# Chunks of the gate and up product: three groups of seven, weight sums by DMA, Silu in one operation

## The chip, the cores and the metric

One core of a Trainium2 chip runs the kernel. Its engines are TensorE (PE), VectorE (DVE), ScalarE (ACT), GpSimd (POOL) and SyncE (SP, which issues most DMAs); each works through its own program in order and waits on semaphores for the others. The metric is the device time of one execution in microseconds; lower is better.

## What is computed

Two transformer layers on 256 tokens of width 2048. Each layer mixes tokens (a sliding window attention in layer 0, a gated recurrence in layer 1, both with attention to 256 memory tokens) and then does a feed-forward step of width 5632, which is what matters here:

```python
x = x + jnp.concatenate([mix, mem_out], axis=-1) @ w_o[i]
gate, up = _split(rms_norm(x, norm_ffn[i]) @ w_gate_up[i], (D_FF, D_FF))
x = x + (jax.nn.silu(gate) * up) @ w_down[i]
```

All is float32.

## The kernel before

**Products.** A float32 product is made of three products of TensorE. Each operand is split in a high part (`_hi`, rounded to what TensorE takes in one pass) and a low part (`_lo`, the rest), and hi times hi, lo times hi and hi times lo are added in PSUM. ScalarE makes `w_hi` by a copy (L644), VectorE makes `w_lo` by a subtraction (L1104).

**Pieces.** Weights come as pieces of 256 rows by 512 columns (512 KB). SyncE loads a piece into one of eight slots of `raw` (`piece`, L411) when the piece eight before is used; `w_hi` has four slots (RING), so ScalarE can split piece n when piece n-4 is used; `w_lo` takes the place of the raw piece. TensorE counts `piece_used`. ScalarE and VectorE run LEAD = 3 pieces ahead: at step i of a loop over pieces they first do the extra work listed for step i and then split piece i+3. A plain piece is 12 products of 128x512 columns (2 row blocks, 3 parts, 2 token tiles; `plain_piece`, L1920).

**Chunks.** The gate and up product (`w_gate_up`) goes in chunks of 512 gate and 512 up columns. The first chunk is done by plain pieces before a loop. The other ten of a layer run in a loop of five turns with two chunks each (`half` 0 and 1). A chunk has 8 quads (row pair q, side 0 gate and side 1 up), thus 16 pieces.

**Groups of seven.** Quads 2 and 5 (SEVEN) are done with seven block products and not eight (`seven_products`, L1901): 21 products of TensorE for 24. It needs forms of the tokens (`seven_forms`, made once a layer, during the first chunk) and four sums of the weight blocks: two in `sums.two`, the third written over block 0 of the raw piece, and the fourth in `sums.all`. `seven_sums` (L1116) makes all four on VectorE; ScalarE waits for them before it splits the quad's first piece. `sums_high` and `sums_low` split the sums. TensorE wants `w_lo` of both pieces before a group, and counts both pieces used at its end.

**Banks.** The plain products and part of the sevens go to four PSUM banks (`own`), the rest of the sevens to the other four (`shared`). In the next chunk the two sets change roles. After the last group, at step 12, ScalarE copies `shared[0]` and both engines move a block of the result of the chunk before into `gT`; at step 13 `shared_products` (L1596) reads the shared banks and gives `own_free`, on which `chunk_products` (L1955) and `down_products` (L1938) wait before their first product. After the last piece `own_products` (L1608) reads the own banks and gives `shared_free`, on which the first group of the next chunk waits.

**Activation.** Silu of the gate is made by Tanh on ScalarE (step 2, L939), one operation for each tile on VectorE (`gate_silu`, step 4, L1581), and `times_up` (step 5, L1585): the product with up and a transpose in 32x32 blocks, which SyncE carries on with 16 small DMAs (`moved`) a chunk.

**GpSimd** makes the factors of the norms, and the masks of the recurrence of layer 1 early in the program. Much of the memory is used twice: `sum_all` is the tile `squares`, `down_two` is the tile `tanh_ff`.

## Time and profile before

| what | value |
|---|---|
| time, median of 3 runs | 2149.47 us (2149.44 to 2149.59) |
| the profiled execution, its own time | 2150.24 us |
| its span, first to last instruction | 2148.5 us |
| TensorE busy | 2135.4 us, 99% of the span |
| VectorE busy | 1682.8 us, 78% |
| ScalarE busy | 1119.4 us, 52% |
| GpSimd busy | 56.6 us, 3% |
| HBM read | 411.25 MB, 192 GB/s over the span |

Busy time tells which engine works most, not which one is waited for. An engine at 99% can only be helped by less work, and one at 78% can still hold the others up where its work comes in a lump. So the busy shares are read first, then windows of one chunk, then the timelines within it.

### The profile page before, as it was taken

The page shows a single profiled execution, that of the slowest core. Times are in us where ns is not written, and L with a number is a line of the kernel's source. Part 1 is how long each engine was busy: PE and PEld are TensorE (multiplying, and loading weights), DVE is VectorE, ACT ScalarE, POOL GpSimd, SP SyncE. Part 2 cuts the span into 40 slices and gives each one's busy share as a digit, 9 for nine tenths or more (in the row PEclk, how much of TensorE's full clock was granted, in tenths as well). Part 3 has the DMA queues.
Part 4 walks back from the last instruction along what each step waited for, and adds up shares of the span by engine and source line. Part 5 has one row for each costly group of instructions (what it writes and reads, how often), then busy time and mean ns, then how long its engine had stood idle before and what let it go on. Part 6 is the DMA issues. An engine that isn't in the chain of part 4 may idle for free.

```text
span 2148.5 us, 29147 instructions
## 1 busy us (share of the span) xinstructions
PE 2135.4 (99%) x9992; PEld 1777.8 (83%) x9992; DVE 1682.8 (78%) x2139; ACT 1119.4 (52%) x1478; POOL 56.6 (3%) x99
## 2 busy tenths in 40 slices
PE   8999999999999999999999999999999999999999
PEld 7888888888888888888888888888888888888887
DVE  6657766898988898777666767667989898898775
ACT  7755654555455555454544544455554555555453
POOL 2101100000000000000000000000000000000000
PEclk9999999999999999999999999999999999999999
DMA  9765467667666766675665656577676667666664
GB/s 327 243 197 147 132 211 207 206 203 227 209 205 201 232 207 211 191 226 180 212 175 158 197 159 199 163 222 205 203 224 210 200 209 227 208 210 202 227 199 138
DMA packets 244568, 435.56 MB, mean 203 GB/s; under 512 B 23040, under 2 KB 43648, under 8 KB 244480
## 3 DMA queue, kind: packets, MB, share of 16 engines
q1 hardware_dynamic: 243392, 432.31, 65.1%
q10 hardware_dynamic: 1088, 2.10, 0.3%
q8 instruction: 52, 0.85, 0.2%
q14 instruction: 36, 0.29, 0.0%
HBM read 411.25 MB, written 2.10 MB: 192 GB/s over the span
## 4 chain that ended last, share of the span: by engine, by line
PE 99%; ACT 0%; DVE 0%; DMA 0%; issue 0%; DVEq 0%; SPq 0%; ACTq 0%
PE unit_bank L1886 30%; PE mix_bank L1928 24%; PE unit_bank L1928 24%; PE mix_bank L1898 7%; PE unit_bank L1898 7%; PE mix_bank L1886 4%; PE mix_bank L1979 1%; PE mix_bank L2109 1%; PE mix_bank L2044 0%; PE mix_bank L2006 0%; PE mix_bank L2053 0%; PE mix_bank L2095 0%; DVE w_lo L1104 0%; PE mix_bank L2017 0%; PE mix_bank L2028 0%; DMA source_T<-in_mem_T 0%
## 5 line engine op out<-in xcount | busy, mean ns | idle before, releaser
L644 ACT ACTIVATE w_hi<-raw 128x1024 fp32r<-128x1024 f32 x767 | 798.1, 1057 | 828.2 <-DVE sum_all L1128 166.5
L1104 DVE TENSOR_TENSOR w_lo<-raw,w_hi 128x1024 fp32r<-128x1024 f32 x767 | 923.4, 1221 | 353.0 <-ACT w_hi L644 346.8
L1886 PE MATMUL unit_bank<-w_hi,hT_hi 128*128 128x512 f32 (+1 forms) x576 | 181.2, 396 | 0.0
L1886 PE MATMUL unit_bank<-w_hi,hT_lo 128*128 128x512 f32 (+1 forms) x576 | 176.2, 387 | 0.0
L1886 PE MATMUL unit_bank<-w_lo,hT_hi 128*128 128x512 f32 (+1 forms) x576 | 175.9, 387 | 0.0
L1928 PE MATMUL unit_bank<-w_lo,hT_hi 128*128 128x512 f32 x480 | 147.9, 389 | 0.0
L1928 PE MATMUL mix_bank<-w_lo,hT_hi 128*128 128x512 f32 x480 | 147.8, 389 | 0.0
L1928 PE MATMUL mix_bank<-w_hi,hT_hi 128*128 128x512 f32 x480 | 147.8, 389 | 0.0
L1928 PE MATMUL unit_bank<-w_hi,hT_hi 128*128 128x512 f32 x480 | 147.8, 389 | 0.0
L1928 PE MATMUL unit_bank<-w_hi,hT_lo 128*128 128x512 f32 x480 | 147.8, 389 | 0.0
L1928 PE MATMUL mix_bank<-w_hi,hT_lo 128*128 128x512 f32 x480 | 147.7, 389 | 0.0
L1886 PEld LDWEIGHTS unit_bank<-w_hi,hT_lo 128*128 128x128 f32 x576 | 107.9, 188 | 21.7
L1886 PEld LDWEIGHTS unit_bank<-w_lo,hT_hi 128*128 128x128 f32 x576 | 107.9, 188 | 21.7
L1886 PEld LDWEIGHTS unit_bank<-w_hi,hT_hi 128*128 128x128 f32 x576 | 104.5, 188 | 18.2 <-DVE w_lo L1104 0.2
L1928 PEld LDWEIGHTS mix_bank<-w_hi,hT_hi 128*128 128x128 f32 x480 | 90.1, 188 | 18.7
L1928 PEld LDWEIGHTS unit_bank<-w_hi,hT_hi 128*128 128x128 f32 x480 | 90.1, 188 | 18.7
L1928 PEld LDWEIGHTS unit_bank<-w_lo,hT_hi 128*128 128x128 f32 x480 | 90.1, 188 | 18.7
L1928 PEld LDWEIGHTS mix_bank<-w_lo,hT_hi 128*128 128x128 f32 x480 | 90.1, 188 | 18.7
L1928 PEld LDWEIGHTS unit_bank<-w_hi,hT_lo 128*128 128x128 f32 x480 | 90.1, 188 | 18.7
L1928 PEld LDWEIGHTS mix_bank<-w_hi,hT_lo 128*128 128x128 f32 x480 | 90.1, 188 | 18.7
L1928 PE MATMUL mix_bank<-w_hi,gT_lo 128*128 128x512 f32 x272 | 83.8, 389 | 0.0
L1928 PE MATMUL unit_bank<-w_hi,gT_lo 128*128 128x512 f32 x272 | 83.8, 389 | 0.0
(427 smaller groups left out, 3602.7 us busy)
## 6 DMA issues: line engine op xcount, KB each, us to landing
raw<-in_w_gate_up SPq DMA_DIRECT2D x352, 512.0 KB, 4.4
raw<-in_w_down SPq DMA_DIRECT2D x176, 512.0 KB, 4.6
raw<-in_w_in_b SPq DMA_DIRECT2D x104, 512.0 KB, 3.7
raw<-in_w_o SPq DMA_DIRECT2D x64, 512.0 KB, 3.8
raw<-in_w_in_a SPq DMA_DIRECT2D x40, 512.0 KB, 3.7
moved<-turned SPq DMA_DIRECT2D x528, 32.0 KB, 2.5
raw<-in_w_mem_kv SPq DMA_DIRECT2D x31, 512.0 KB, 5.5
tanh_ff<-act_ff SPq DMA_DIRECT2D x112, 32.0 KB, 3.0
```

The costliest lines, as they stand in the source:

```text
L644: act.activation(w_hi[:, s, :, :], raw[:, r, :, :], ACT.Copy).then_inc(sems["hi_ready"], 1)
L1104: dve.tensor_tensor(w_lo[:, r, :, :], raw[:, r, :, :], w_hi[:, s, :, :].bitcast(F32), ALU.subtract).then_inc(sems["lo_ready"], 1)
L1886: ins = pe.matmul(all_banks[2 * pair + tile][:, 0:cols], stationary[part][:, kt + j, tile * P:(tile + 1) * P], b[:, j, 0:cols], start=open ...
L1898: ins = pe.matmul(bank[:, :], x_parts[part], w, start=start and m == 0, stop=stop and m == 2)
L1928: ins = pe.matmul(own[2 * tile + side][:, :], x[part][:, kt + j, tile * P:(tile + 1) * P], w, start=opens and j == 0 and m == 0, stop=clos ...
L1979: ins = pe.transpose(mix_bank[b][:, n * P:(n + 1) * P], src[:, n * width:(n + 1) * width], ident[:, :])
L2109: ins = pe.matmul(mix_bank[b][:, h * P:(h + 1) * P], early_key[:, h, :], whole(query_in, h * P + half, (4 * P - half, TILES), (size, block ...
```

## The change

- SEVEN is (2, 4, 6): three groups of seven in a chunk, and a chunk ends with one plain quad. The order of the row pairs is QUAD_KTS, so that the third group has rows 10 and 11.
- Two of a group's four weight sums are no longer made by VectorE. SyncE loads block 0 into both halves of a `two` tile (`spread`, two DMAs of 256 KB), GpSimd issues two DMAs that add another block onto them (`chunk_weight_sums`). The tile exists twice now, and groups take turns. Of the quad's first piece only the lower half is loaded into `raw`.
- VectorE makes the third sum (`third_sum`) and the fourth (`fourth_sum`), both a step later than `seven_sums` did. ScalarE waits for the third before its split and for the fourth before `sums_high`.
- The work that follows the last group goes from steps 12 and 13 to 14 and 15 (LAST_SEVEN).
- Silu is one operation of ScalarE; `gate_silu` of VectorE is gone. The half factors are gone too.
- The forms of the third group (`late_form`) are made at steps 11 and 12 of the first chunk, in memory that the masks have later; GpSimd makes the masks between layer 0 and layer 1 instead, and the recurrence waits for them (`masks_ready`).
- SyncE waits for the forms (`own_free`) before it starts on the loop.

```diff
--- before.py
+++ after.py
 LEAD = 3
 LEVELS = 7
+OWN_FREED = CHUNKS_FF + 2
 QUAD_PIECES = 2
 CHUNK_PIECES = KT
-SEVEN = (2, 5)
-SEVEN_APART = 6
+SEVEN = (2, 4, 6)
+SEVEN_APART = 4
+QUAD_KTS = (0, 2, 4, 6, 8, 12, 10, 14)
+SPREAD_STEPS = (1, 5, 13)
+LAST_SEVEN = 2 * SEVEN[-1] + 2
 SEVEN_PIECES = tuple(2 * q for q in SEVEN)
...
+        late_forms = tuple(at(f"late_forms_{n}", [3, P], F32R, place[0] - LEVELS * SEQ // 2 * 4 + m * 3 * P * 4)
+                           for m, n in enumerate(("hi", "lo")))
...
-        chunk_sums = Sums(sums, sums_lo, sum_all, sum_all_lo, sums_hi)
+        chunk_sums = tuple(Sums(two, two_lo, sum_all, sum_all_lo, sums_hi)
+                           for two, two_lo in ((sums, sums_lo), (down_two, down_two_lo)))
+        chunk_forms = [tuple(f[:, g, :, :] for f in forms) for g in range(2)]
+        chunk_forms.append(tuple(f[:, :, :] for f in late_forms))
...
+        def chunk_sum(half, n):
+            return (half * len(SEVEN) + n) % 2
...
+            def lower_half_piece(w, kt, col):
+                s = slot[0] % RAW
+                slot[0] += 1
+                t.move("piece_used")
+                sp.wait_ge(sems["piece_used"], t.value("piece_used", RAW))
+                sp.dma_start(raw[:, s, 1, :], w[(kt + 1) * P:(kt + 2) * P, bass.ds(col, COLS)]).then_inc(sems[f"arrived{s}"], 16)
+
+            def spread(w, kt, col, b, used):
+
+                sp.wait_ge(sems["piece_used"], t.value("piece_used", used))
+                for m in range(2):
+                    sp.dma_start(chunk_sums[b].two[:, m, :], w[kt * P:(kt + 1) * P, bass.ds(col, COLS)]).then_inc(sems[f"spread{b}"], 16)
...
+                before = [2 * q + 2 - CHUNK_PIECES for q in SEVEN] + [2 * q + 2 for q in SEVEN]
+                spread_after = [before[len(SEVEN) + m - 2] for m in range(len(SEVEN))]
...
+                sp.wait_ge(sems["own_free"], layer * OWN_FREED + 1)
                 with t.loop(0, CHUNKS_FF // 2, {"piece_used": 2 * CHUNK_PIECES, "turned_ready": 2}) as j:
                     for half in range(2):
+                        col = j * (2 * COLS) + (1 + half) * COLS
                         for n in range(CHUNK_PIECES):
-                            piece(wg, n // 2 * 2, j * (2 * COLS) + (1 + half) * COLS + n % 2 * D_FF)
+                            load = lower_half_piece if n in SEVEN_PIECES else piece
+                            load(wg, QUAD_KTS[n // 2], col + n % 2 * D_FF)
+                            if n in SPREAD_STEPS:
+                                m = SPREAD_STEPS.index(n)
+                                spread(wg, QUAD_KTS[SEVEN[m]], col, chunk_sum(half, m), n + 1 - spread_after[m])
                             chunk_turns(n)
...
+            def chunk_weight_sums(layer):
+
+                w = w_gate_up[layer, :, :]
+                with t.loop(0, CHUNKS_FF // 2, {f"spread{b}": 32 * len(SEVEN) for b in range(2)}) as j:
+                    for half in range(2):
+                        col = j * (2 * COLS) + (1 + half) * COLS
+                        for n, q in enumerate(SEVEN):
+                            kt, b = QUAD_KTS[q], chunk_sum(half, n)
+                            pool.wait_ge(sems[f"spread{b}"], t.next(f"spread{b}", 32))
+                            pool.dma_start(chunk_sums[b].two[:, 0, :], w[(kt + 1) * P:(kt + 2) * P, bass.ds(col, COLS)],
+                                           accum_op=ALU.add).then_inc(sems[f"summed{b}"], 16)
+                            pool.dma_start(chunk_sums[b].two[:, 1, :], w[kt * P:(kt + 1) * P, bass.ds(col + D_FF, COLS)],
+                                           accum_op=ALU.add).then_inc(sems[f"summed{b}"], 16)
...
+                def gate_silu():
                     for s in range(TILES):
                         act.wait_ge(sems["gate_sum"], t.next("gate_sum"))
-                        act.activation(tanh_ff[:, s, :], act_ff[:, s, :], ACT.Tanh,
-                                       scale=half_rs[:, s:s + 1]).then_inc(sems["tanh_ff_ready"], 1)
-
-                def chunk(j, shared):
+                        act.activation(act_ff[:, s, :], act_ff[:, s, :], ACT.Silu,
+                                       scale=rs[:, s:s + 1]).then_inc(sems["silu_ready"], 1)
+
+                def chunk(j, half, shared):
                     for i in pieces(CHUNK_PIECES):
                         if i + LEAD in SEVEN_PIECES:
-                            act.wait_ge(sems["sum_ready"], t.next("sum_ready", 3))
+                            act.wait_ge(sems["sum_ready"], t.next("sum_ready"))
                         if i + LEAD - 2 in SEVEN_PIECES:
-                            sums_high(chunk_sums)
+                            act.wait_ge(sems["sum_ready"], t.next("sum_ready"))
+                            sums_high(chunk_sums[chunk_sum(half, SEVEN_PIECES.index(i + LEAD - 2))])
                         if i == 2:
-                            gate_tanh()
-                        if i == 12:
+                            gate_silu()
+                        if i == LAST_SEVEN:
                             act.wait_ge(sems["piece_used"], t.value("at"))
                             act.activation(up_ff[:, 0, :], shared[0][:, :], ACT.Copy).then_inc(sems["first_copied"], 1)
-                        if i == 12:
+                        if i == LAST_SEVEN:
                             moved_block(gT, j * 4)
...
+            def third_sum(sums, b):
+
+                r = slot[0] % RAW
+                blocks = four_blocks(raw, r)
+                dve.wait_ge(sems[f"summed{b}"], t.next(f"summed{b}", 32))
+                dve.wait_ge(sems[f"arrived{r}"], t.value(f"arrived{r}", -16))
+                dve.tensor_tensor(blocks[:, 0, :], sums.two[:, 1, :], blocks[:, 1, :], ALU.add).then_inc(sems["sum_ready"], 1)
+
+            def fourth_sum(sums, used):
+
+                r = slot[0] % RAW
+                blocks = four_blocks(raw, r)
+                dve.wait_ge(sems["piece_used"], t.value("at", used))
+                dve.wait_ge(sems[f"arrived{r + 1}"], t.value(f"arrived{r + 1}", -16))
+                dve.wait_ge(sems["sum_ready"], t.next("sum_ready"))
+                dve.tensor_tensor(sums.all[:, :], blocks[:, 0, :], blocks[:, 3, :], ALU.add).then_inc(sems["sum_ready"], 1)
+                dve.wait_ge(sems["sum_ready"], t.next("sum_ready"))
...
                 def times_up():
-                    dve.wait_ge(sems["dve_chain"], t.next("dve_chain"))
                     dve.wait_ge(sems["shared_free"], t.value("shared_free"))
                     for s in range(TILES):
+                        dve.wait_ge(sems["silu_ready"], t.next("silu_ready"))
                         ins = dve.scalar_tensor_tensor(out=up_ff[:, s, :], in0=up_ff[:, s, :],
-                                                       scalar=half_rs2[:, s:s + 1], in1=tanh_ff[:, s, :], op0=ALU.mult,
+                                                       scalar=rs[:, s:s + 1], in1=act_ff[:, s, :], op0=ALU.mult,
                                                        op1=ALU.mult)
...
-                def chunk(j, own, shared):
+                def chunk(j, half, own, shared):
 
                     for i in pieces(CHUNK_PIECES):
-                        if i + LEAD + 1 in SEVEN_PIECES:
-                            seven_sums(chunk_sums)
+                        if i + LEAD in SEVEN_PIECES:
+                            n = SEVEN_PIECES.index(i + LEAD)
+                            b = chunk_sum(half, n)
+                            third_sum(chunk_sums[b], b)
+                            fourth_sum(chunk_sums[b], i - (2 * SEVEN[n - 1] + 2) if n else 0)
                         if i + LEAD - 2 in SEVEN_PIECES:
-                            sums_low(chunk_sums)
-                        if i == 4:
-                            gate_silu()
+                            sums_low(chunk_sums[chunk_sum(half, SEVEN_PIECES.index(i + LEAD - 2))])
                         if i == 5:
                             times_up()
-                        if i == 12:
+                        if i == LAST_SEVEN:
                             moved_block(gT, j * 4, "gT_ready")
-                        if i == 13:
+                        if i == LAST_SEVEN + 1:
                             shared_products(shared)
                     own_products(own)
...
-                    if i == 10:
+                    if i == 9:
                         seven_forms()
+                    if i == 11:
+                        seven_forms_lo()
+                        late_form()
                     if i == 12:
-                        seven_forms_lo()
+                        late_form_lo()
...
-            def chunk_products(own, shared):
+            def chunk_products(half, own, shared):
 
                 pe.wait_ge(sems["own_free"], t.next("own_free"))
                 for q in range(CHUNK_PIECES // 2):
                     if q in SEVEN:
                         n = SEVEN.index(q)
-                        seven_products(hT, 2 * q, forms, n, chunk_sums, own, shared, n == 0, n == len(SEVEN) - 1, evicted)
+                        seven_products(hT, QUAD_KTS[q], chunk_forms[n], chunk_sums[chunk_sum(half, n)], own, shared, n == 0, n == len(SEVEN) - 1, evicted)
                         continue
                     for side in range(2):
-                        plain_piece(hT, 2 * q, side, own, q == 0, q == CHUNK_PIECES // 2 - 1)
+                        plain_piece(hT, QUAD_KTS[q], side, own, q == 0, q == CHUNK_PIECES // 2 - 1)
...
```

In `seven_products` only the arguments are other. `late_form` is one operation of 512 columns and four of 128 on VectorE, and `late_form_lo` two more.

## Rows read from the trace of the kernel before

**Rows 1.** The page: its head, and busy time by engine.
```profile
span 2148.5 us, 29147 instructions
...
PE 2135.4 (99%) x9992; PEld 1777.8 (83%) x9992; DVE 1682.8 (78%) x2139; ACT 1119.4 (52%) x1478; POOL 56.6 (3%) x99
```

**Rows 2.** Windows: stretch, length, busy of PE, PEld, DVE, ACT, POOL; PEclk, DMA, GB/s.
```profile
414.19:456.35 42.16, 42.16 (x188) 34.91 (x186) 37.38 (x43) 21.84 (x25) 0.00 (x0) 1.00 0.69 213
```

**Rows 3.** Timeline, TensorE, one chunk: start, length, engine, line, operation, count.
```profile
429.83 0.62 PE L1928 MATMUL mix_bank<-w_hi,hT_hi 128*128 128x512 f32 x2
...
440.71 0.39 PE L1898 MATMUL mix_bank<-w_hi,hT_hi 128*128 128x512 f32 x1
...
445.47 0.62 PE L1928 MATMUL mix_bank<-w_hi,hT_hi 128*128 128x512 f32 x2
...
456.35 0.62 PE L1928 MATMUL unit_bank<-w_hi,hT_hi 128*128 128x512 f32 x2
```

**Rows 4.** Timeline, VectorE, the same chunk.
```profile
429.61 1.41 DVE L1589 SCALAR_TENSOR_TENSOR up_ff<-up_ff,half_rs,tanh_ff 128x512 f32<-128x512 f32 x2
432.28 1.18 DVE L1104 TENSOR_TENSOR w_lo<-raw,w_hi 128x1024 fp32r<-128x1024 f32 x1
433.39 1.22 DVE L1123 TENSOR_TENSOR sums<-raw 128x1024 f32<-128x1024 f32 x1
434.64 0.69 DVE L1126 TENSOR_TENSOR raw<-sums,raw 128x512 f32<-128x512 f32 x1
435.37 0.69 DVE L1128 TENSOR_TENSOR sum_all<-raw 128x512 f32<-128x512 f32 x1
...
446.76 1.23 DVE L1104 TENSOR_TENSOR w_lo<-raw,w_hi 128x1024 fp32r<-128x1024 f32 x1 [2.98 <-ACT w_hi L644]
447.90 1.29 DVE L1209 TENSOR_TENSOR gT_lo<-moved,gT_hi 128x512 f32 x2
449.23 1.23 DVE L1104 TENSOR_TENSOR w_lo<-raw,w_hi 128x1024 fp32r<-128x1024 f32 x1
450.37 0.68 DVE L1600 TENSOR_TENSOR act_ff<-unit_bank,up_ff 128x512 f32<-128x512 f32 x1
452.42 0.69 DVE L1605 TENSOR_TENSOR act_ff<-unit_bank,up_ff 128x512 f32<-128x512 f32 x1
...
456.63 1.29 DVE L1613 TENSOR_TENSOR act_ff<-mix_bank,act_ff 128x512 f32<-128x512 f32 x2
```

**Rows 5.** Groups by line, whole span: busy us, mean ns, idle before.
```profile
L1134 DVE TENSOR_TENSOR sums_lo<-sums,sums_hi 128x1024 fp32r<-128x1024 f32 x40 | 49.0, 1226 | 5.9 <-ACT sums_hi L658 4.8
...
L1581 DVE SCALAR_TENSOR_TENSOR tanh_ff<-tanh_ff,act_ff 128x512 f32<-128x512 f32 x44 | 28.3, 686 | 0.0
```

**Rows 6.** Timeline, ScalarE, the same chunk.
```profile
445.67 1.06 ACT L644 ACTIVATE w_hi<-raw 128x1024 fp32r<-128x1024 f32 x1 [3.70 <-PE mix_bank L1898]
...
447.11 1.15 ACT L707 ACTIVATE gT_hi<-moved 128x512 f32 x2
```

**Rows 7.** Start of the span: window of the first products; timeline, two rows.
```profile
7.98:13.24 5.26, 5.26 (x12) 4.12 (x13) 3.95 (x8) 4.01 (x8) 0.00 (x0) 1.00 1.03 408
...
7.14 0.69 DVE L1440 TENSOR_TENSOR w_lo<-raw,w_hi 128x512 fp32r<-128x512 f32 x1
...
7.98 1.19 PE L1886 MATMUL unit_bank<-w_hi,memT_hi 128*128 128x512 f32 x2 [7.98 <-DVE w_lo L1440]
```

**Rows 8.** SyncE's queue: timeline; DMA issues by size; landings of line 432.
```profile
430.16 0.99 SPq L417 DMA_DIRECT2D raw<-in_w_gate_up  x2
...
raw<-in_w_mem_kv SPq DMA_DIRECT2D x2, 256.0 KB, 3.8
...
DMA to landing us min/median/max: 1.8/2.6/5.4
```

**Rows 9.** Timeline, GpSimd: its longest operation and a small one.
```profile
232.37 2.90 POOL L581 TENSOR_TENSOR head_rs<-head_ms,minus_half 128x16 f32<-128x16 f32 x1
...
1052.87 1.11 POOL L579 TENSOR_SCALAR head_ms<-head_ss 128x8 f32<-128x8 f32 x1 [21.52 <-DVE head_ss L1214]
```

108 lines of the change are left out of this document (63 added, 45 removed).

## The prediction

> **What bounds the kernel now.** I read the page first: TensorE is busy for 2135.4 of 2148.5 us, VectorE for 78% and ScalarE for 52% [rows 1]. A busy TensorE can still be waiting, so I then cut one half turn of the chunk loop out with the windows view. In 42.16 us TensorE has no idle time at full granted clock, VectorE is busy 37.38 us, ScalarE 21.84, and the DMA engines 0.69 at 213 GB/s [rows 2]. The timeline of TensorE gives the borders [rows 3]: four plain pieces take 440.71 - 429.83 = 10.88 us (48 products, 0.2267 us each), a group of seven takes 445.47 - 440.71 = 4.76 us (21 products), and the last four plain pieces 10.88 us. A chunk is 186 products, 186 x 0.2267 = 42.16 us. So here the number of products sets the time, and the other engines matter only where one of their chains is longer than the TensorE work that covers it. Those chains are what I looked for next, in the timelines of VectorE and ScalarE.
>
> The execution I work from has a span of 2148.5 us [rows 1] and a time of its own of 2150.24 us, so 1.7 us lie around the span; the median of the three runs, 2149.47, is 0.8 us (0.04%) below it. The change leaves what is around the span alone, so the differences from this execution are added to the median.
>
> **What is taken away.** A third group of seven replaces the two plain pieces of one quad: 21 products for 24, in 20 chunks (10 a layer). That is 3 x 0.2267 = 0.68 us a chunk and 13.6 us in all, on the path. A chunk would need 183 x 0.2267 = 41.48 us.
>
> **VectorE's balance.** Per chunk it loses two sums of 1024 columns (433.39 to 434.64, 1.25 us each [rows 4]) and two silu operations of 0.69 [rows 5]: some 3.8 us. It gains for the third group two sums of 512 columns (0.73 us each [rows 4]) and the low halves (1.23 [rows 5] and one more of 512 columns, about 0.6): 3.3 us. So 37.4 becomes about 36.9 of 41.48 us: no bound by quantity. ScalarE gains one pair of sums_high, some 1.6 us by the same sizes, on 21.8, and changes Tanh for Silu at the same shape. Neither counts. What counts is order.
>
> **First new wait: the banks at the end of a chunk.** The two halves of PSUM change roles: what was `shared` in one chunk is `own` in the next, and `chunk_products` waits on `own_free` before its first product. VectorE gives `own_free` with the last operation of `shared_products` (L1605), which can only start after the last group of seven. Before, the last group (q=5) is followed by four plain pieces, 10.88 us of cover. After, SEVEN ends in 6: two plain pieces, 24 x 0.2267 = 5.44 us. `moved_block` and `shared_products` move with it, from steps 12 and 13 to 14 and 15, in the same order. I call G the start of the piece behind the last group, 445.47 [rows 3]. ScalarE may split the piece four behind the group's first only now (ring of four), at 445.67 [rows 6]. VectorE's low half of it starts at 446.76, then the two gT_lo operations at 447.90 (they need ScalarE's from 447.11 [rows 6]), the next low half at 449.23, the four sums of shared_products from 450.37, the last starting at 452.42 and taking 0.69: done at 453.11 = G + 7.64 [rows 4]. VectorE stood idle before 446.76, so this chain hangs on G, not on a backlog, and it moves with the group. From VectorE's result to TensorE's first product I take 0.15 us: L1440 ends at 7.14 + 0.69 = 7.83, TensorE starts at 7.98 [rows 7]. So the next chunk starts at G + 7.79 and not at G + 5.44: **2.35 us of idle TensorE a chunk**. It comes after each of 20 chunks, since `down_products` waits on `own_free` too. Bounds: 2.2 (no latency) to 2.6 us.
>
> **Second new wait: the ninth piece.** The groups are now at pieces 4, 8 and 12. At step 5 VectorE does third_sum and fourth_sum for piece 8, then `times_up` (two products, two transposes), then the low half of piece 8, and at step 6 that of piece 9. `sum_all` exists once, and `fourth_sum(..., i - (2*SEVEN[n-1]+2))` gives -1 here: it waits until the first group (pieces 4, 5) is used. Everything named stands behind it in VectorE's order. Call that time T, 429.83 [rows 3]. VectorE is known to start 456.63 - 456.35 = 0.28 us after such an event [rows 3, 4]. Then: fourth_sum 0.73 (435.37 minus 434.64), times_up and transposes 432.28 - 429.61 = 2.67, low half of piece 8 433.39 - 432.28 = 1.11, and that of piece 9 with its full length, 1.23 [rows 4]: T + 6.02, with the latency T + 6.17. TensorE has two plain pieces to do, 5.44 us, and then wants both halves at once (`lo_ready` by 2). **0.73 us of idle TensorE a chunk.** In the kernel before, times_up began at 429.61, before T. Bounds: 0.3 (VectorE starts and TensorE wakes at once) to 1.0. At the third group (step 9) the same wait costs nothing: without times_up, VectorE needs 0.28 + 0.73 + 1.11 + 1.23 = 3.35 of 5.44 us.
>
> **The adding DMAs.** No row shows a DMA issued by GpSimd or one that adds. Their deadline is tightest for the third group: SyncE can issue pieces 12 and 13 only at T (430.16, two in 0.99 us [rows 8]), then two spreads of 256 KB, until about T + 2.4; a 256 KB load landed in 3.8 us at the busy start [rows 8], so T + 5.8. GpSimd waits for that, and issues two DMAs. VectorE must begin third_sum by T + 12.0: the group starts at T + 6.17 + 4.76 + 5.44 = T + 16.37, and before it lie third_sum 0.7, two ScalarE splits of about 1.0, the last low half 1.23 and 0.15, or 4.2 with the hand-overs. That leaves 6.2 us. From below: one GpSimd operation of 1.11 and a landing of 1.8; from above: two of 2.90 and a landing of 5.4, 11.2 us, late by 5 us a chunk [rows 8, 9]. I take 1 us for each issue (the small one, since only an issue is queued and nothing computed) and a landing like the load's 3 to 4: 5 to 6 us, just in time, at no cost. A miss costs its full length 20 times, since VectorE stands at third_sum with all splits behind it. The first and second groups have over 5 us more.
>
> The Trainium skill (DMA: Bandwidth & Descriptors, Anatomy of one DMA) puts a GpSimd DMA at about 2.0 us plus the bytes at 436 GB/s, an estimate of 2.6 us for 256 KB; by it the sums would be in time too. It also says that adding is left to GpSimd's DMAs, and no run here shows either yet.
>
> The bytes: a chunk moves 16 x 512 KB = 8.4 MB now; it gains 3 x 3 x 256 KB net (two spreads and two adds less the half that isn't loaded), 2.4 MB, and the adds read their target also, 1.6 MB. 12.4 MB in 44.5 us is 280 GB/s; the first microseconds ran at 408 [rows 7]. Not a bound.
>
> **Around the loop.** The extra form (`late_form`) lies in steps 11 and 12 of the plain chunk with over 1 us to spare each; the new wait of SyncE on `own_free` delays the first loads of the loop, 0 to 0.5 us a layer. The masks moved on GpSimd are 28 small operations, by the small one [rows 9] at most 31 us, and are wanted 17 pieces, 46 us, into the group that follows. I take 0.5 us for all, 0 to 3.
>
> **Sum.** Per chunk 2.35 + 0.73 - 0.68 = +2.40 us, times 20 = +48.0, plus 0.5: 2149.5 + 48.5 = **2198 us**, 2.3% slower. The period should be 44.56 us instead of 42.16. Bounds of the two waits alone: 2.5 to 3.6 a chunk, 2186 to 2208.
>
> **Rivals.**
> 1. The adding DMAs are late. The same sum plus 20 times the miss: at 1 us 2218, at 2.5 us 2248, at the upper bound 2298. For it: 6.2 us for two unseen operations. Against it: spare DMA bandwidth.
> 2. The cover holds after all (the faster side). The mechanism is the chain behind the last group: if VectorE gave the banks back within 5.3 us instead of 7.64, and times_up ran before the wait, the gain of 0.68 a chunk stays: 2149.5 - 13.6 = 2136. It turns at waits of 0.68 us a chunk in sum. Against it: neither order is in the diff. With only the second wait left, 2149.5 + 20 x (0.73 - 0.68) = 2150, no change.
> 3. TensorE's clock falls after the 2.35 us holes. After its first idle 7.98 us twelve products took 5.26 us, 0.44 each instead of 0.23, as at 1.2 GHz, though the column reads 1.00 [rows 7]. If every hole cost that again, 5.26 - 12 x 0.2267 = 2.5 us a chunk: 2198 + 51 = 2249. Behind that start all holes of the span sum to 2148.5 - 7.98 - 2135.4 = 5.1 us, so its rows can't tell what a hole of 2.35 us does, and the first one was over three times as long. The skill's page TensorE: Matmul & The Clock Gate (Part 1) says that an idle array drops to the lower clock and regains it by work; by it this rival would need holes longer than mine.
> 4. GpSimd is held off by VectorE while it makes its DMAs. That is rival 1 with another cause. The skill (SBUF — State Buffer, Door 1 to 3, the trap under them) describes descriptor making that stops while VectorE copies in a two-port mode; the loop has no such copy, so by the page there is nothing, and no row here shows it.
>
> **How the numbers follow.** Forecast (both waits, DMAs in time) 0.60. DMAs late 0.27, of it half below 2230. Clock 0.05. Only one of the two waits (2183 or 2150) 0.05, cover holds 0.03. Range: from 2186, just under the bounds of the forecast, to 2250, which takes in the clock rival and late DMAs up to 2.5 us; left out are some 0.08 below and 0.08 above. A difference under 0.2% (4.3 us) can't be told from none. Faster by more: 0.03; within: 0.03; slower: 0.94.
>
> **What the profile after would show.** TensorE idle of 2.3 us before the first product of each chunk, released by L1605's successor (act_ff or up_ff of shared_products), 20 times; idle of 0.7 us before the middle group, released by w_lo, 20 times; period 44.6 us; clock 1.00; VectorE near 83% of a period. If third_sum waits on a DMA with TensorE idle before the third group, rival 1 holds, and its length is the miss. If the period is 41.5, I have misread who waits for the banks. A period between 41.5 and 44 would say that one chain is shorter than its rows.

## The result and the profile after

The changed kernel takes **2320.7 us** (median of 4 runs, 2319.4 to 2327.8) where the kernel before takes 2149.5: a ratio of 1.080, 95% interval 1.079 to 1.082. Slower was forecast, but 2198 us, with a range of 2186 to 2250. So the sign was right and 123 us are missing from the sum.

The page of the changed kernel, head, busy time and the queue of GpSimd's DMAs (packets, MB, share):

```profile
span 2317.7 us, 30023 instructions
...
PE 2182.6 (94%) x9932; PEld 1789.3 (77%) x9932; DVE 1675.1 (72%) x2149; ACT 1174.7 (51%) x1543; POOL 161.2 (7%) x215
...
q0 software_dynamic: 17280, 31.46, 8.8%
```

Against [rows 1], TensorE's busy time went up by 47.2 us though it has 60 products less, which should have saved 13.6: **60.8 us of slower products**, at a lower clock or at the edges of holes. Its idle time went from 13.1 to 135.1: **122.0 us of new holes**. Together 122.0 + 60.8 - 13.6 = 169.2, all that the span grew by. Where the holes are, by the view of TensorE's waits (us in total, times, longest):

```profile
PE unit_bank L1989 <- DVE w_lo L1159: 44.7, 22, 7.2
PE mix_bank L1989 <- DVE w_lo L1159: 33.1, 20, 3.6
PE unit_bank L2019 <- DVE act_ff L1670: 21.7, 10, 2.3
PE mix_bank L2019 <- DVE act_ff L1670: 21.6, 10, 2.2
```

L2019 is the plain product and L1670 the last operation of `shared_products`: the wait for the banks, 43.3 us in 20. L1989 is the group of seven: 77.8 us in 42. One chunk tells them apart, in the timelines of TensorE, VectorE, SyncE and GpSimd:

```profile
430.10 0.73 PE L2019 MATMUL mix_bank<-w_hi,hT_hi 128*128 128x512 f32 x2 [2.15 <-DVE act_ff L1670]
...
432.18 1.06 PE L2019 MATMUL mix_bank<-w_hi,hT_hi 128*128 128x512 f32 x2
433.04 1.06 PE L2019 MATMUL mix_bank<-w_hi,hT_lo 128*128 128x512 f32 x2
...
453.62 0.50 PE L1989 MATMUL mix_bank<-w_hi,hT_hi 128*128 128x512 f32 x1 [0.55 <-DVE w_lo L1159]
...
467.05 0.50 PE L1989 MATMUL mix_bank<-w_hi,hT_hi 128*128 128x512 f32 x1 [2.94 <-DVE w_lo L1159]
...
481.34 0.72 PE L2019 MATMUL unit_bank<-w_hi,hT_hi 128*128 128x512 f32 x2 [2.17 <-DVE act_ff L1670]
```
```profile
447.75 0.69 DVE L1201 TENSOR_TENSOR sum_all<-raw 128x512 f32<-128x512 f32 x1 [1.93 <-PE mix_bank L1989]
...
462.74 0.69 DVE L1192 TENSOR_TENSOR raw<-down_two,raw 128x512 f32<-128x512 f32 x1 [5.17 <-DMA down_two<-in_w_gate_up]
```
```profile
448.94 0.82 SPq L443 DMA_DIRECT2D down_two<-in_w_gate_up  x2
```
```profile
454.17 0.87 POOL L624 DMA_DIRECT2D down_two<-in_w_gate_up  x1 [20.92 <-DMA down_two<-in_w_gate_up]
454.81 1.12 POOL L626 DMA_DIRECT2D down_two<-in_w_gate_up  x1
```

The chunk lasts 481.34 - 430.10 = 51.24 us where 44.56 were forecast. The hole of 2.17 us at its end and that of 0.55 before the middle group were forecast. The hole of **2.94 us before the third group** was not, nor were the products 0.43 us apart from 431.3 to 434.2 (432.18 to 433.04 are two). With T = 447.46, the first group's end: the spreads go out at T + 1.5, GpSimd starts at T + 6.7 and ends at T + 8.5, VectorE gets the sums at T + 15.3. The deadline was T + 12.0. TensorE's row names `w_lo` only because it waits for that; VectorE itself stands for 5.17 us at `third_sum`, on the DMA.

The granted clock, by the windows view (length, busy of PE, PEld, DVE, ACT, POOL, PEclk, DMA, GB/s), shows the slow stretches of this chunk behind its two long holes, and none behind the short one:

```profile
430.10:442.70 12.60, 12.60 (x48) 10.28 (x49) 10.89 (x13) 5.77 (x7) 1.76 (x2) 0.86 0.79 207
...
453.62:458.51 4.89, 4.89 (x21) 4.05 (x22) 3.95 (x4) 0.54 (x1) 1.77 (x2) 1.00 0.62 134
...
467.05:471.60 4.55, 4.55 (x13) 3.58 (x14) 4.10 (x4) 1.86 (x2) 0.51 (x1) 0.65 1.03 379
```

At the two levels a product takes 0.2267 and 0.427 us (2.4 and 1.2 GHz). Not every long hole has slow products behind it. In TensorE's timeline of the whole span 25 of the 62 holes in the loops have them: 12 of the 20 at the banks, 11 of the 20 before the third group, and both at the loops' entries; of the 20 of 0.55 and 0.65 us none has. Where they follow, they are 5 to 11 and cost some 1.7 us, 41 us in sum. Most of the other 20 of the 60.8 us are the edges of the 62 holes: the product before a hole and the one behind it take 0.3 us more together.

### The profile page after: what moved, and what is told of

It is laid out like the page before. It is cut to its first block, busy times and chain, and to the rows that moved or that the text cites. A ratio compares the mean times of both kernels' runs of the same rounds, so it can differ in the third digit from the quotient of the medians.

```text
span 2317.7 us, 30023 instructions
## 1 busy us (share of the span) xinstructions
PE 2182.6 (94%) x9932; PEld 1789.3 (77%) x9932; DVE 1675.1 (72%) x2149; ACT 1174.7 (51%) x1543; POOL 161.2 (7%) x215
## 3 DMA queue, kind: packets, MB, share of 16 engines
q0 software_dynamic: 17280, 31.46, 8.8%
## 4 chain that ended last, share of the span: by engine, by line
PE 71%; DMA 11%; issue 5%; DVE 5%; ACT 4%; SPq 2%; ACTq 0%; DVEq 0%; POOLq 0%; POOL 0%
PE unit_bank L1977 27%; PE mix_bank L2019 14%; PE unit_bank L2019 11%; DMA sums<-in_w_gate_up 7%; PE unit_bank L1989 7%; PE mix_bank L1989 7%; DMA down_two<-in_w_gate_up 4%; PE mix_bank L1977 3%; ACT w_hi L692 2%; DVE w_lo L1159 2%; PE mix_bank L2070 1%; ACT gT_hi L755 1%; PE mix_bank L2200 1%; DVE raw L1192 1%; DVE act_ff L1665 1%
## 5 line engine op out<-in xcount | busy, mean ns | idle before, releaser
L2019 PE MATMUL mix_bank<-w_hi,hT_hi 128*128 128x512 f32 x400 | 128.5, 403 | 21.6 <-DVE act_ff L1670 21.6
L2019 PE MATMUL unit_bank<-w_hi,hT_hi 128*128 128x512 f32 x400 | 125.8, 396 | 17.8 <-DVE act_ff L1670 17.5
L2019 PE MATMUL mix_bank<-w_hi,hT_lo 128*128 128x512 f32 x400 | 127.7, 402 | 0.0
L2019 PE MATMUL mix_bank<-w_lo,hT_hi 128*128 128x512 f32 x400 | 126.8, 399 | 0.0
L2019 PE MATMUL unit_bank<-w_hi,hT_lo 128*128 128x512 f32 x400 | 125.3, 395 | 0.0
L2019 PE MATMUL unit_bank<-w_lo,hT_hi 128*128 128x512 f32 x400 | 124.9, 394 | 0.0
L1977 PEld LDWEIGHTS unit_bank<-w_hi,hT_lo 128*128 128x128 f32 x576 | 107.9, 188 | 21.8
L1977 PEld LDWEIGHTS unit_bank<-w_hi,hT_hi 128*128 128x128 f32 x576 | 104.4, 188 | 18.2 <-DVE w_lo L1159 0.2
L2019 PEld LDWEIGHTS mix_bank<-w_hi,hT_hi 128*128 128x128 f32 x400 | 76.8, 194 | 41.5 <-issue 25.8
L2019 PEld LDWEIGHTS unit_bank<-w_hi,hT_hi 128*128 128x128 f32 x400 | 75.2, 190 | 37.3 <-issue 20.8
L2019 PEld LDWEIGHTS mix_bank<-w_lo,hT_hi 128*128 128x128 f32 x400 | 78.2, 195 | 16.9
L2019 PEld LDWEIGHTS mix_bank<-w_hi,hT_lo 128*128 128x128 f32 x400 | 77.7, 194 | 16.8
L2019 PEld LDWEIGHTS unit_bank<-w_lo,hT_hi 128*128 128x128 f32 x400 | 76.5, 191 | 16.2
L2019 PE MATMUL unit_bank<-w_hi,gT_hi 128*128 128x512 f32 x272 | 84.8, 393 | 4.2 <-DVE act_ff L1670 4.2
L2019 PEld LDWEIGHTS unit_bank<-w_hi,hT_lo 128*128 128x128 f32 x400 | 76.1, 190 | 16.1
L2019 PE MATMUL unit_bank<-w_lo,gT_hi 128*128 128x512 f32 x272 | 85.1, 394 | 0.0
```

The source lines that it names most:

```text
L1977: ins = pe.matmul(all_banks[2 * pair + tile][:, 0:cols], stationary[part][:, kt + j, tile * P:(tile + 1) * P], b[:, j, 0:cols], start=open ...
L2019: ins = pe.matmul(own[2 * tile + side][:, :], x[part][:, kt + j, tile * P:(tile + 1) * P], w, start=opens and j == 0 and m == 0, stop=clos ...
```

## The experiments

The kernel before ran beside each of them (medians 2150.1 to 2150.4).

**Remove one suspected cause at a time.** In e1 the third group's four sums are VectorE's again and its piece is loaded whole; the other groups keep the adding DMAs:

```diff
-SPREAD_STEPS = (1, 5, 13)
+SPREAD_STEPS = (1, 5)
+BY_DMA = len(SPREAD_STEPS)
...
-                            third_sum(chunk_sums[b], b)
+                            if n < BY_DMA:
+                                third_sum(chunk_sums[b], b)
+                            else:
+                                two_sums(chunk_sums[b])
```

> The changed kernel, but the third group's four weight sums are made by VectorE as before (its first piece is loaded whole, no spreads and no adding DMAs for it; groups one and two keep theirs). Theory A (adding DMAs late for the third group only, 3.3 us a chunk by the idle of TensorE before the third group, and about half of the slow clock behind that hole): 2321 - 20 x 3.3 - about 23 = 2230 us, no idle of TensorE before the third group, the holes of 2.2 us (banks) and 0.6 us (middle group) stay. Theory B (GpSimd's DMAs disturb everything, by their bytes or by holding VectorE): four of six remain, so only a third of the excess goes, some 2290 us. Theory C (the VectorE work that comes back, 1.25 us a chunk, opens a new wait): above 2235 us with VectorE busy in front of the third group.

Measured: 2258.6 us (1.050, 1.048 to 1.051), 62 less: between theories A and B. It has no hole before the third group, and those at the banks and before the middle group stay. What theory A missed is new: ten holes before the first group, 15.3 us in sum, and 17.3 us at the loops' entries for 13.5. GpSimd now leaves up to 8.1 us between the two adding DMAs of a pair, 99.5 us in 15 pairs; this comes back in e4.

In e2 `shared_products` comes ahead of gT's block:

```diff
                         if i == LAST_SEVEN:
+                            shared_products(shared)
+                        if i == LAST_SEVEN + 1:
                             moved_block(gT, j * 4, "gT_ready")
-                        if i == LAST_SEVEN + 1:
-                            shared_products(shared)
```

> The changed kernel with two steps of VectorE swapped at the end of a chunk: shared_products (which gives the banks back) at step 14 and the gT move at step 15. Theory A (TensorE waits for the banks because the chain behind the last group is 7.64 us against 5.44 us of cover): the chain becomes 7.64 - 1.33 - 1.14 = 5.2 us plus 0.15 latency, so the hole of 2.2 us goes 20 times, 47 us, and the slow clock behind it, about 23: 2250 us. If the clock does not hang on this hole: 2274 us. Rival (VectorE or the adding DMAs are the bound and the banks' hole would be filled by a later wait): under 10 us of gain, above 2310 us.

Measured: 2295.7 us (1.066, 1.063 to 1.069), only 25 less; its own rival (above 2310) falls too. The view of waits says where the rest went:

```profile
PE unit_bank L1989 <- DVE w_lo L1159: 66.6, 30, 6.7
PE mix_bank L1989 <- DVE w_lo L1159: 41.9, 30, 3.0
```

The 43.3 us at the banks are gone, but the waits before groups of seven grew from 77.8 to 108.5, with 18 new ones: a hole in front of the first group (0.9 and 2.4 us in two chunks). It seems that the hole at the banks had given VectorE and the DMAs time for that group.

In e3 `times_up` stands between the third and the fourth sum; in the change it stands behind both:

```diff
                             third_sum(chunk_sums[b], b)
+                            if i == 5:
+                                times_up()
                             fourth_sum(chunk_sums[b], i - (2 * SEVEN[n - 1] + 2) if n else 0)
...
-                        if i == 5:
-                            times_up()
```

> The changed kernel with times_up between third_sum and fourth_sum at step 5, so that it runs before the wait for the first group and not behind it. Theory A (waits follow each other in one chain: the adding DMAs of the third group start at T, when the first group is used, and land at T + 15.3 whatever happens between): the hole before the middle group, 0.6 us, goes, and the one before the third group grows by as much: no change, 2320 us within 5. Rival (the holes simply add): 20 x 0.7 = 14 us less, 2307 us.

Measured: 2300.5 us (1.070, 1.067 to 1.073). The waits on `w_lo` fall from 77.8 to 65.8 us, the 20 holes of 0.6. It gained 20 us, more than the 12 of the holes and more than both theories, though one of its four runs (2294.4 to 2307.7) lies at the rival's 2307. The holes before the third group are hardly longer for it (53 us for 52), so theory A's one chain is wrong and the rival, that the holes add, is right. The other 7 us are TensorE's busy time: some 6 by the edges of 20 holes at 0.3, and little by the clock (193 slow products for 201).

e4 has all three edits:

> All three edits: the third group's sums on VectorE, shared_products before the gT move, times_up before the wait. Theory A (two orders and one late transfer explain the whole loss, and the slow clock follows from the holes): no holes in the loop, granted clock 1.00, and the gain in products is left: 2149.5 - 13.6 + 0 to 3 = 2136 to 2139 us. Rival (the third group costs more on VectorE than the three products save, or the clock falls for another reason): 2150 us or more.

Measured: 2239.9 us (1.042, 1.040 to 1.044), a miss by 100 us. The holes at the banks and before the third group are gone and those before the middle group are down to 0.2 us, but another stands there, 51.2 us in 10 waits before the first group, the two at the loops' entries (5.84 and 11.03 us) among them; in the other chunk of a turn it is 0.9 to 2.7 us. Timelines of GpSimd and VectorE, and GpSimd's waits:

```profile
461.51 0.87 POOL L625 DMA_DIRECT2D sums<-in_w_gate_up  x1 [31.04 <-DMA sums<-in_w_gate_up]
468.80 0.86 POOL L627 DMA_DIRECT2D sums<-in_w_gate_up  x1 [6.42 <-issue]
```
```profile
474.89 0.69 DVE L1204 TENSOR_TENSOR raw<-sums,raw 128x512 f32<-128x512 f32 x1 [2.09 <-DMA sums<-in_w_gate_up]
```
```profile
POOL sums L627 <- issue: 58.1, 9, 7.6
POOL down_two L627 <- issue: 44.0, 10, 5.9
```

GpSimd gives out the second adding DMA of a pair 6.4 us after the first ends, with nothing to wait for. That is 102 us in 19 of 40 pairs.

**Take the DMAs, or only the adding, away.** In e5 VectorE makes all sums; it is e4 with

```diff
-SPREAD_STEPS = (1, 5)
+SPREAD_STEPS = ()
...
-            chunk_weight_sums(0)
...
-            chunk_weight_sums(1)
```

> The changed kernel with all three reorderings of the run e4_all_three, and no adding DMA at all: VectorE makes the four weight sums of all three groups from pieces that are loaded whole. Theory A (in e4_all_three only the adding DMAs of the first two groups are left as a cause of holes, and the holes as the cause of the lower clock): no hole, 183 products of 0.2267 us a chunk, about 2138 us (2134 to 2146), TensorE busy 2122. Rival B (VectorE, about 41 us of work in 41.5, becomes the bound once it makes all sums): 2160 or more, with holes released by w_lo and none of VectorE's own waits on DMAs.

Measured: 2243.5 us (1.043, 1.042 to 1.045). Rival B holds: without one adding DMA it is no faster than e4. Now VectorE is late for the first group, in part because it waits for ScalarE's split behind silu:

```profile
475.65 1.28 ACT L986 ACT_TABLE_LOAD   x1
476.94 1.33 ACT L986 ACTIVATE act_ff<-act_ff,rs 128x512 f32<-128x512 f32 x2
```
```profile
479.25 1.22 DVE L1158 TENSOR_TENSOR w_lo<-raw,w_hi 128x1024 fp32r<-128x1024 f32 x1 [2.37 <-ACT w_hi L691]
```

e6 is e4, and e7 the changed kernel, with the addition left out of the same DMAs:

```diff
-                            pool.dma_start(chunk_sums[b].two[:, 0, :], w[(kt + 1) * P:(kt + 2) * P, bass.ds(col, COLS)],
-                                           accum_op=ALU.add).then_inc(sems[f"summed{b}"], 16)
+                            pool.dma_start(chunk_sums[b].two[:, 0, :], w[(kt + 1) * P:(kt + 2) * P, bass.ds(col, COLS)]).then_inc(sems[f"summed{b}"], 16)
```

> e4_all_three with GpSimd's DMAs plain copies and not adding (the two sums then lack their first block). Theory A (adding is what makes the transfer slow): the landing falls from about 6 to about 3.6 us and VectorE finds the sums ready: some 2195 to 2210. Rival B (GpSimd gives the second DMA of a pair out 3 to 7 us after the first, whatever it does): the gap between the two stays, 2230 to 2240.

> The changed kernel itself with GpSimd's DMAs plain copies and not adding (the sums lack their first block). Theory A (adding makes the landing 5 to 7 us, and that is the hole before the third group): landing near 3.6, the hole of 2.9 us falls to under 1 and part of the slow products after it goes: 2235 to 2270. Rival B (the chain is long by the order of its steps and the busy queues, not by the addition): less than 15 us gained, above 2305.

Measured: e6 2208.7 us (1.027, 1.025 to 1.029), 31 less than e4, and the 6 us gaps are gone (0.6 us from one DMA to the next). e7 2243.8 us (1.044, 1.043 to 1.046), 77 less; of the 20 holes before the third group 3 are left, 3.2 us in sum. The bytes from HBM are the same, so the addition as such costs, in both. Its price, by the DMA issues of 400 to 900 us in e7 (count, KB, median us to landing), and by its page:

```profile
sums<-in_w_gate_up POOLq DMA_DIRECT2D x28, 256.0 KB, 3.5
down_two<-in_w_gate_up POOLq DMA_DIRECT2D x28, 256.0 KB, 3.7
...
q0 software_dynamic: 9600, 31.46, 4.3%
```

In the changed kernel the same two rows say 5.4 and 5.3, the packets are 17280 for the same bytes, and one issue takes 0.87 to 1.09 us where a plain one takes 0.56.

e8 is the kernel before with the work behind the last group two steps later on both engines, as in the change (VectorE's part):

```diff
-                        if i == 12:
+                        if i == 14:
                             moved_block(gT, j * 4, "gT_ready")
-                        if i == 13:
+                        if i == 15:
                             shared_products(shared)
```

> The kernel before, with gT's block at step 14 and shared_products at step 15 and nothing else: the first wait by itself, at 186 products a chunk. The hole should be the 2.2 to 2.4 us of the changed kernel. Theory A (a hole costs its own length only): 2149.5 + 20 x 2.3 = 2195. Theory C (each such hole also lowers TensorE's clock for the next products, as the 8 products 0.427 us apart in the changed kernel suggest, 8 x 0.2 = 1.6 us): 2195 + 32 = 2227.

Measured: 2180.6 us (1.014, 1.012 to 1.016), below both. The hole is 1.22 us, not 2.3. The last group is two pieces earlier here, so VectorE's chain need not wait for its end; that is argued from the order, not tried. All 20 cost 30 us, 1.5 each, and the clock stays at 1.00: a hole of this length costs itself and some 0.3 us in the products at its edges. What a hole of 2.3 us does to the clock, the question between the two theories, e8 can't say.

**Silu.** e12 is the kernel before with silu in one operation and nothing else; e14 has it at step 1, before ScalarE's wait for the first group's sums:

```diff
+                        if i == 1:
+                            gate_tanh()
                         if i + LEAD in SEVEN_PIECES:
                             act.wait_ge(sems["sum_ready"], t.next("sum_ready", 3))
...
-                        if i == 2:
-                            gate_tanh()
```

> The kernel before with silu in one operation of ScalarE and no gate_silu on VectorE, and nothing else. Theory A (this part is off the path, as forecast): 2149 to 2151. Rival B (the loads of ScalarE's table, two a turn, delay the fifth piece as in e5_no_adding): 2155 or more.

> e12_silu_alone with silu at step 1, ahead of ScalarE's wait for the first group's sums. Theory A (the 6.6 us of e12_silu_alone are the 10 holes of 0.4 us released by the fifth piece, behind table load and silu): 2150 to 2152, equal to the kernel before. Rival B (silu on ScalarE costs in another way): still 2155 or more.

Measured: e12 2156.9 us (1.003, 1.002 to 1.004), so 6.6 us lost, and e14 2150.4 us (1.000, 0.999 to 1.001), none. With Tanh ScalarE loads no table in the loop. With Silu it has two loads a turn, each 1.28 us, 20 in all: one right before silu, one before a split near the turn's end. At step 2 the first lies, with silu, between the splits of pieces 4 and 5. The Trainium skill (ScalarE: Activation LUTs, What ACT_TABLE_LOAD costs) says some 1283 ns for the load and 1380 ns more for a drain; the trace agrees with the first and shows no drain, since silu starts at once after the load, as in e5's rows.

**Repairing VectorE's order.** e10 is e5 with silu at step 4; e11 gives the middle group's two sums back to adding DMAs; e9 adds gT's block at step 13 in the first chunk of each turn; e13 has silu at step 1 instead of 4.

```diff
-                        if i == 2:
+                        if i == 4:
                             gate_silu()
...
-                        if i == LAST_SEVEN + 1:
+                        if i == (LAST_SEVEN + 1 if half else LAST_SEVEN - 1):
                             moved_block(gT, j * 4, "gT_ready")
```

> e5_no_adding with ScalarE's silu at step 4 and not at step 2, that is behind the splits of the first group's two pieces. In e5_no_adding a load of ScalarE's table (1.28 us) and two silu operations (1.33 in sum) stand between the splits of pieces 4 and 5, and VectorE waits 2.37 us for the second, in one of two chunks. Theory A (that wait is part of the hole before the first group): the holes of 3.6 and 2.2 us there become 1.4 and 1.0, with less lost to the clock: 2200 to 2222. Rival B (VectorE has too much work between the last group and the first, and silu's place is nothing): above 2235.

> e10_silu_later, with the two sums of the middle group alone given back to SyncE's spreads and GpSimd's adding DMAs; the first and third group stay with VectorE. Theory A (an adding DMA is harmless where its group has over 10 us of time, and takes 1.2 us from VectorE just where it is late): the hole of 1.4 us before the middle group goes, 25 us less than e10_silu_later, 2170 to 2195. Rival B (the adding DMAs also stall here, 6 us between the two of a pair): no gain on e10_silu_later.

> e11_middle_by_dma, with gT's block at step 13 in the first of a turn's two chunks (in the second its memory is still used by the sums), where VectorE stands idle for 2.9 us behind the third group. Theory A (VectorE's backlog between the third group and the next first group is the hole): 1.2 us less in 10 of 20 chunks, 8 to 12 us below e11_middle_by_dma. Rival B (the hole before the first group hangs on ScalarE or a DMA): the same as e11_middle_by_dma within 3 us.

> e9_eased with ScalarE's silu at step 1, ahead of its wait for the first group's sums, where ScalarE stands idle for 7 us in every chunk. Theory A (silu and the table load before it delay the seventh piece, then times_up, in one of two chunks, and so make the hole of 1.65 us before the middle group): that hole goes, 10 x 1.6 us less, 2165 to 2172. What is left is the hole of 1.2 us before the first group in one of two chunks. Rival B (the holes of the second chunk of a turn come from VectorE's backlog alone): 2180 to 2186.

Measured: e10 2234.6 (1.040, 1.038 to 1.041), e11 2194.6 (1.021, 1.019 to 1.022), e9 2184.0 (1.015, 1.014 to 1.017) and e13 2167.3 us (1.008, 1.006 to 1.009). For e10 the gain is only 9 us, near its rival: silu moved the lateness on to the middle group (2.9 us in one of two chunks). The other three are in theory A's ranges, e11 with a gain of 40 us where 25 were named. In e13 only 12.0 us of holes before groups are left, and still a chunk without one lasts 42.0 us and not 41.48. Before its middle group, with VectorE's low halves for it last:

```profile
565.68 0.61 PE L2034 MATMUL unit_bank<-w_lo,hT_hi 128*128 128x512 f32 x2
566.27 0.50 PE L2004 MATMUL unit_bank<-w_hi,hT_hi 128*128 128x512 f32 x1
566.61 0.39 PE L2004 MATMUL unit_bank<-w_hi,hT_lo 128*128 128x512 f32 x1
```
```profile
563.86 2.36 DVE L1160 TENSOR_TENSOR w_lo<-raw,w_hi 128x1024 fp32r<-128x1024 f32 x2
```

Two products should take 0.45 us and take 0.59, and the next takes 0.34 for 0.23: 0.25 us lost at the border without idle time in the rows. The trace says why: the second low half ends at 566.22 and TensorE starts at 566.27, 0.05 us behind it, so this is a short wait for `w_lo`. From 380 to 800 us in e13 every border before a first or middle group is like this, while before the third group the low half is ready 0.95 us early or more and nothing is lost.

**Repairing SyncE's order.** e15 is the changed kernel with one number changed, so that the third group's spreads go out ahead of pieces 12 and 13:

```diff
-SPREAD_STEPS = (1, 5, 13)
+SPREAD_STEPS = (1, 5, 11)
```

> The changed kernel, with the third group's spreads issued by SyncE ahead of pieces 12 and 13 and not behind them. Theory A (the chain spread, landing, adding DMAs, landing is the hole before the third group, link by link): about 1 us less of a hole of 2.9 us in 20 chunks, 2320.7 - 20 to - 40 = 2281 to 2301. Rival B (the landings depend on what else moves at that time, so an earlier issue lands no earlier): above 2312.

Measured: **2233.7 us** (1.039, 1.037 to 1.040), 87 less. One window of a whole chunk, and the links in the timelines of SyncE, GpSimd and VectorE:

```profile
426.14:470.94 44.80, 42.08 (x183) 34.19 (x184) 36.85 (x43) 24.40 (x28) 5.27 (x6) 1.00 0.86 251
```
```profile
442.25 0.82 SPq L443 DMA_DIRECT2D down_two<-in_w_gate_up  x2
```
```profile
446.25 0.87 POOL L624 DMA_DIRECT2D down_two<-in_w_gate_up  x1 [15.01 <-DMA down_two<-in_w_gate_up]
```
```profile
453.78 0.69 DVE L1192 TENSOR_TENSOR raw<-down_two,raw 128x512 f32<-128x512 f32 x1 [1.75 <-DMA down_two<-in_w_gate_up]
```

T is 441.92 here: issue at T + 0.3, GpSimd at T + 4.3, sums at T + 11.9. The issue is 1.2 us sooner and the end 3.4, and all 20 holes before the third group are gone. The spreads, no longer behind the 768 KB of the two pieces, landed in 4.0 us for 5.2, and the adding DMAs in 5.8 for 6.8, though they are still issued behind those pieces. So neither theory is quite right: the chain holds link by link, but its landings depend on the place in the queue. TensorE's idle time fell by 52.5 us and its busy time by 32.6, with 8 holes that slow products follow for 25.

e16 has the repairs of e2, e3 and e15, silu at step 1, and the first group's spreads ahead of the chunk's first piece; e17 is e4 with the last two.

```diff
+                        spread(wg, QUAD_KTS[SEVEN[0]], col, chunk_sum(half, 0), -spread_after[0])
                         for n in range(CHUNK_PIECES):
```

> The changed kernel with every repair that the runs so far point to, all three groups' sums still by adding DMAs: shared_products ahead of gT, times_up ahead of the fourth sum, silu at step 1, and the spreads of the first and third group issued ahead of the pieces that come free with them. Theory A (order is all that was wrong): no hole over 0.5 us, 183 products of 0.2267 us a chunk, 2136 to 2148, faster than the kernel before. Rival B (with the holes at a chunk's start gone, GpSimd's second adding DMA of a pair is given out 6 us late, as in e4_all_three, and the first group waits for it): 2170 to 2230.

> e4_all_three with silu at step 1 and the first group's spreads issued ahead of the chunk's first piece. Theory A (the first group's sums came late because its spreads stood behind two pieces in SyncE's order, and silu did the rest): the hole of 5 us before the first group goes, 2136 to 2150. Rival B (the gap of 6 us between the two adding DMAs of the first pair stays whatever SyncE does): at least half of the loss stays, above 2185.

Measured: e16 2182.4 (1.015, 1.014 to 1.017) and e17 2176.5 us (1.013, 1.011 to 1.014). e16 is in its rival's range, but not by its mechanism: GpSimd issues both DMAs of every pair at once. There all adding DMAs land later (medians 7.4 and 6.8 us from 400 to 900 us), and small holes remain; that they meet more pieces is my guess. e17 lies between the theories: the gaps between two adding DMAs are still there, 141 us in sum, but mostly hidden.

No version beats the kernel before. e14, with its two groups of seven, equals it.

## Why the prediction missed

**TensorE as the bound, and the gain of three products.** The bound was right. The gain of 0.68 us a chunk was sized for a chunk without any waiting; the best chunks of e13 show 42.0 to 42.1 for 42.16, a gain of 0.1, and the rest went to the short waits for `w_lo`.

**The banks.** 2.35 us a chunk was forecast and a hole of 2.17 (43.3 us in 20) came, at the place and by the releaser named. The idle time of a row is less than the delay: from the start of the last product (478.78) to that of the next (481.34) it is 2.56 us for 0.23, a delay of 2.33. The chain read off [rows 4] held to 0.02 us.

**The ninth piece.** 0.73 us forecast, holes of 0.55 and 0.65 seen in two chunks (delays of 0.72 and 0.81), and 12.0 us of holes taken away by e3. Right.

These two and the gain give the period that was forecast where the adding DMAs are in time and the clock stays up: the chunk of e15 above lasts 44.80 us against 44.56, and the next, at whose start the clock fell, 46.50.

**The adding DMAs: the step that failed.** "A landing like the load's 3 to 4" was the choice, from one row of 256 KB at the start of the span [rows 8]; it was 6.8 us. The landing before it was 4.4 to 5.2 for 3.8, in a queue with two pieces ahead. GpSimd's two issues took 1.8 us for 2. Together T + 15.3 for T + 11 to 12. Either half repaired is enough: plain DMAs (e7) or spreads issued sooner (e15) take this hole away. Of the 77.8 us before groups, 13.5 belong to the loop's entry (below) and some 12 to the middle group: the third group's holes are 52 us, 2.6 a chunk. The working had an upper bound that held (5 us late) and took the low end as its choice; rival 1 had a chance of 0.27. No row of the kernel before spoke for an addition at the price of a plain load.

The Trainium skill (DMA: Bandwidth & Descriptors, Anatomy of one DMA) gave an estimate of 2.6 us for 256 KB. The plain DMAs of e7 took 3.5 to 3.7 beside the kernel's other traffic and the adding ones 5.3 to 7.4, so the trace disagrees, by over a third for the plain ones and by a factor of two and more for the adding ones.

**The clock: rival 3, given 0.05.** It was worked out at 2.5 us behind each of 20 holes; it came behind 25 of 62, 12 of them at the banks, at 1.7 us, some 41 us in sum. Its chance was set by the first hole being three times as long, and no row spoke for that as a reason. The rival had the mechanism, and the sum lacked it as a second price on the holes: that is most of why e15 gained 87 us for 52 of holes. The sum was right to lack it in part, since 8 of the 20 holes at the banks had no slow product behind them; what decides it stays open. The unforeseen holes (52 and 13.5) and the slower products (60.8), less the 6 by which the idle time of the two forecast holes is smaller than their forecast delays, are 120 of the 123 us.

**Around the loop.** 0.5 us forecast, up to 3. SyncE's wait on `own_free` holds the loop's first pieces and spreads, and the first group's sums come late: holes of 7.23 and 6.30 us at the two entries, 13.5 us, and about 1.5 and 2.6 of slow products behind them. What I had left out is that the first group's spreads stand behind that wait too. In e16, where they go out first and silu is earlier, 1.8 us of holes are left at each entry up to the first group, and 2.3 before the middle group at one; no run tries the spreads' place alone.

**Silu at nothing.** It was costed as the same shape as Tanh. In the kernel before, silu with its table loads cost 6.6 us (e12) and nothing at another step (e14). What it costs inside the changed kernel was not tried alone.

**GpSimd held off.** Rival 4 saw a gap that isn't in the changed kernel (3.7 us in all) but is in e4 and e17, 102 and 141 us. It is in e1 too (99.5 us). It comes with two adding pairs a chunk, not with one (e13) and little with three (19.7 us in e15, none in e16), and not with plain DMAs (e6). VectorE runs the same kinds of operations in all of these, which speaks against it as the cause; no run isolates it, and the cause stays open.

## What to carry to other kernels

Price a DMA by a row of its own kind and in the queue where it will stand; if there is none, put the forecast on the slow end of the bounds, and issue the transfer with the tightest deadline ahead of the bulk loads that come free with it. When a change opens holes in a busy TensorE, give those of some 2 us and more a second price for the clock (here 1.7 us, behind about every other one), and when one is closed ask which engine had been using it. A function of ScalarE with another table belongs where ScalarE waits anyway.

## What the hardware showed

- A 256 KB adding DMA of GpSimd: 144 packets for 80, 5.3 to 7.4 us to landing for 3.5 to 4.4, 0.9 to 1.1 us to issue for 0.56. The times to landing are medians. With two pairs a chunk, up to 8.3 us between the issues of one pair (e17).
- Whether a hole lowers the granted clock goes with its length, but not with that alone. Slow products followed none of the 20 holes of 1.2 us in e8 and all holes of 3.2 us and more (10 in e4, 10 in e5). Behind holes of 2.1 to 2.3 us at the banks they came in 12 of 20 in the changed kernel and in 6 of 20 in e15. A fall costs about 1.7 us in these two, and up to 2.9 in e4. Here is one, in e15:

```profile
470.94:476.60 5.66, 5.66 (x18) 4.53 (x19) 5.63 (x8) 0.42 (x1) 1.74 (x2) 0.70 1.12 289
```

- A product of TensorE that waits for an operand can be late without idle time in its row: a border where `w_lo` was ready 0.05 us before the start cost 0.25 us in e13, one where it was ready 0.95 us before cost nothing.
- The Trainium skill (TensorE: Matmul & The Clock Gate, Part 1) says that an idle array drops to the lower clock. The trace agrees, and shows it at holes shorter than I had read into the page.
